# RWKV-7 inverse: the middle products of levels 0 to 3 as sixteen 32x32 blocks in four row sets instead of eight 64x64 blocks in two quarters

## The reference, cut to what matters

```
def step(S, inp):
    r_t, w_t, k_t, v_t, a_t, b_t = inp
    sa = jnp.einsum('bhvk,bhk->bhv', S, a_t)
    S = S * w_t[:, :, None, :] + sa[..., None] * b_t[:, :, None, :] + v_t[..., None] * k_t[:, :, None, :]
    y = jnp.einsum('bhvk,bhk->bhv', S, r_t)
    return S, y
```

## Time and profile before

| | |
|---|---|
| median of three runs | 1392.73 us |
| profiled execution, its time | 1392.75 us |
| its span | 1390.6 us |
| TensorE busy | 1362.9 us, 98% |
| VectorE busy | 855.2 us, 61% |
| ScalarE busy | 696.2 us, 50% |
| line 2782 (the middle products), busy in the core | 25.9 us, 640 records |

### The profile page before, as it was taken

The page is one execution under the profiler, slowest core; times in us unless marked ns, Lnnn a source line. Parts: engine busy times, 40 slices in busy tenths (PEclk is TensorE's granted clock), DMA queues, the critical chain, the costliest instruction groups (busy, mean ns, idle before and its releaser), DMA issues.

```text
span 1390.6 us, 23783 instructions
## 1 busy us (share of the span) xinstructions
PE 1362.9 (98%) x8927; PEld 1118.7 (80%) x8927; DVE 855.2 (61%) x1234; ACT 696.2 (50%) x1110; POOL 38.1 (3%) x42
## 2 busy tenths in 40 slices
PE   9999999999999999999999999899999999999998
PEld 7888877878888878888787688778888887788887
DVE  5455568876755464445784788665555677655554
ACT  5444456675465554444554454235444566644442
POOL 0000000000000000000001000110000010000000
PEclk9999999999999999999999999999999999999999
DMA  8655546555444566555352101315555651266552
GB/s 292 217 181 181 181 145 209 161 191 197 163 158 164 148 203 204 195 183 181 124 187 86 52 4 33 112 46 167 183 192 183 227 174 55 80 214 194 182 184 103
DMA packets 145536, 220.25 MB, mean 158 GB/s; under 512 B 16760, under 2 KB 65294, under 8 KB 145328
## 3 DMA queue, kind: packets, MB, share of 16 engines
q1 hardware_dynamic: 145456, 219.14, 48.4%
HBM read 218.04 MB, written 1.05 MB: 158 GB/s over the span
## 4 chain that ended last, share of the span: by engine, by line
PE 89%; DVE 6%; ACT 3%; issue 1%; POOL 1%; DVEq 0%; POOLq 0%; ACTq 0%
PE acc L291 12%; PE gp L291 12%; PE acc L293 12%; PE acc L292 12%; PE gp L293 12%; PE gp L292 12%; PE tp L952 1%; PE gp L2782 1%; PE acc L2797 1%; DVE sb_w_lo L280 1%; PE acc L1295 1%; PE tp L291 1%; PE tp L293 1%; PE tp L292 1%; PE gp L1884 1%
## 5 line engine op out<-in xcount | busy, mean ns | idle before, releaser
L280 DVE TENSOR_TENSOR sb_w_lo<-sb_raw,sb_w_hi 128x1024 fp32r<-128x1024 f32 (+1 forms) x380 | 451.5, 1214 | 205.2 <-ACT sb_w_hi L264 203.4
L264 ACT ACTIVATE sb_w_hi<-sb_raw 128x1024 fp32r<-128x1024 f32 (+1 forms) x380 | 387.7, 1053 | 207.8 <-PE acc L293 105.9
L291 PE MATMUL gp<-sb_w_hi,sb_xa_hi 128*128 128x512 f32 (+1 forms) x752 | 298.4, 397 | 3.6 <-DVE sb_w_lo L280 2.2
L293 PE MATMUL gp<-sb_w_lo,sb_xa_hi 128*128 128x512 f32 (+1 forms) x752 | 291.7, 388 | 0.0
L292 PE MATMUL gp<-sb_w_hi,sb_xa_lo 128*128 128x512 f32 (+1 forms) x752 | 291.2, 387 | 0.0
L291 PEld LDWEIGHTS gp<-sb_w_hi,sb_xa_hi 128*128 128x128 f32 x752 | 141.3, 188 | 35.7 <-DVE sb_w_lo L280 4.5
L293 PEld LDWEIGHTS gp<-sb_w_lo,sb_xa_hi 128*128 128x128 f32 x752 | 141.2, 188 | 29.6
L292 PEld LDWEIGHTS gp<-sb_w_hi,sb_xa_lo 128*128 128x128 f32 x752 | 141.5, 188 | 27.2 <-issue 0.5
L291 PE MATMUL acc<-sb_w_hi,sb_mid_hi 128*128 128x512 f32 x400 | 156.2, 390 | 0.0
L293 PE MATMUL acc<-sb_w_lo,sb_mid_hi 128*128 128x512 f32 x400 | 155.8, 390 | 0.0
L292 PE MATMUL acc<-sb_w_hi,sb_mid_lo 128*128 128x512 f32 x400 | 155.7, 389 | 0.0
(11 more groups left out here) (417 smaller groups left out, 1758.3 us busy)
## 6 DMA issues: line engine op xcount, KB each, us to landing
sb_raw<-in_ffn_w SPq DMA_DIRECT2D x264, 256.0 KB, 4.4
sb_raw<-in_mlp_w SPq DMA_DIRECT2D x256, 256.0 KB, 2.9
sb_raw<-in_w_in SPq DMA_DIRECT2D x72, 256.0 KB, 3.3
sb_raw<-in_a_w_rkv SPq DMA_DIRECT2D x48, 256.0 KB, 4.1
sb_raw<-in_xattn_w_kv SPq DMA_DIRECT2D x32, 256.0 KB, 3.7
sb_raw<-in_w_out SPq DMA_DIRECT2D x16, 256.0 KB, 3.1
sb_raw<-in_xattn_w_q SPq DMA_DIRECT2D x16, 256.0 KB, 3.0
sb_raw<-in_xattn_w_o SPq DMA_DIRECT2D x16, 256.0 KB, 3.0
```

Of the source, the lines that this page charges most:

```text
L264: A.e.activation(w_hi[:, s, :, 0:n], raw[:, r, :, 0:n], ACT.Copy).then_inc(hi_done, 1)
L280: V.e.tensor_tensor(w_lo[:, s, :, 0:n], raw[:, r, :, 0:n], w_hi[:, s, :, 0:n].bitcast(F32), ALU.subtract).then_inc(lo_done, 1)
L291: e.matmul(dst, xh, wh, start=start, stop=False)
L293: return e.matmul(dst, xh, wl, start=False, stop=stop)
```

## The change: what it does

At level n the mask wants only entries inside diagonal blocks of 2^(n+2), at most 32 for n = 0 to 3. So for these levels only the two 32x32 blocks on the diagonal of each 64x64 product are computed. Each needs only 32 input partitions. `pe_z` then issues sixteen matmuls of 32x32x32 where it issued eight of 64x64x64; in turn they read partitions 0, 64, 32 and 96 onwards and write 64, 0, 96 and 32 onwards. Level 4, whose blocks are 64 wide, is as before. The blocks off the diagonal in `gp` keep what was there; ScalarE still copies all 256 columns, and the masks drop what comes of them. No other instruction is changed.

```diff
+BLOCK = P // 4
...
+            def crossed_blocks(self):
+
+                for col in range(0, HALF, BLOCK):
+                    for at, there in self.crossed():
+                        yield slice(at.start + col, at.start + col + BLOCK), slice(there.start + col, there.start + col + BLOCK), col
...
                 for m in range(4):
-                    for at, there in self.crossed():
-                        mm = T.e.matmul(gp[there, s, m * HALF:(m + 1) * HALF], self.mt[s][at, m, 0, there], self.x_inv[s][at, m, :], start=True, stop=True)
+                    if n < LEVELS - 1:
+                        for at, there, col in self.crossed_blocks():
+                            mm = T.e.matmul(gp[there, s, m * HALF + col:m * HALF + col + BLOCK], self.mt[s][at, m, 0, there],
+                                            self.x_inv[s][at, m, col:col + BLOCK], start=True, stop=True)
+                    else:
+                        for at, there in self.crossed():
+                            mm = T.e.matmul(gp[there, s, m * HALF:(m + 1) * HALF], self.mt[s][at, m, 0, there], self.x_inv[s][at, m, :], start=True, stop=True)
                 mm.then_inc(*T.one(self.z[s]))
```

## The result

The kernel after took 1396.86 us (median of seven runs, 1395.37 to 1398.65), the kernel before 1392.75 (seven runs, 1392.54 to 1395.92). Ratio 1.0024, 95% interval 1.0015 to 1.0033: slower. The forecast was 1389.6 with a range of 1388.4 to 1393.0, and slower had a chance of 0.09. The profiled execution of after took 1395.37, span 1393.2, mean granted clock 0.994.

What follows compares the result with a forecast made beforehand. TensorE was taken as the bound, busy 98% of the span. Savings of 0.44 (unit 0), 2.04 (passes 1 to 4), 0.27 (5 and 6) and 0.43 (7) sum to 3.2 us: 1389.6, range 1388.4 to 1393.0.

Steps and rivals of the forecast that it cites:

- The product: Middle product of levels 0 to 3 on TensorE: 0.46 us instead of 0.68, next shape after 0.39 instead of 0.61.
- the floor: Rival: a short matmul's interval stays that of 64 columns, so nothing is saved; 1392.7 us (to 1393.0), 20%.
- the row sets: Rival: 32x32 tiles in different row sets do not run side by side; +9 us, 1402, 8%.
- The places: Saving at each changed product of a pass, by which wait ends last: 0.54 us a pass, 3.2 us in all.
- Unit 0: First unit, alone with three products: two save in full, the third nothing; 0.44 us saved.
- z(u, 0): Level 0 product in front of level 4's: saves nothing, since xy(3, 0) waits for the second fill-in.
- Levels 2 and 3: Level 2, before the columns, saves 0.22 us a pass; level 3, between pairs and rhs, saves 0.17.
- passes 5 and 6: VectorE's group norm comes between and most of the saving is lost; 0.27 us left for both together.
- pass 7: Last pass: 0.21 us at z(7, 1), nothing at z(7, 2), 0.22 at z(7, 3); 0.43 saved.
- the instruction supply: Rival: 512 more records shift the fetches; a second or doubled stop gives 1390.6 us, none 1388.5; 8% for the first.
- the stop of the earlier trace: TensorE's 0.84 us standstill without a wait in xy(7, 1), DMA engines full; read as a late instruction fetch.
- level 1: Product z(u, 1), followed by u_first and xy(u, 1): saves 0.15 of 0.22 us a pass.

Runs made afterwards that it cites:

- e4: Kernel before with the 32x32 blocks at level 0 only, weight loads not held: 1392.70 us, ratio 1.0001.
- e12: Kernel after with blocks only at levels 2 and 3, and the weight loads held until y of unit 6 is done: 1389.75 us, ratio 0.9976.
- e8: Kernel before, with only the weight loads held until y of unit 6 is done: 1391.92 us, ratio 0.9987.
- e3: Kernel after, all four levels in blocks, with the weight loads held until y of unit 6 is done: 1391.38 us, ratio 0.9982.
- e7: e3 plus 64 small matmuls (256 instructions) in one 32x32 corner at the head of TensorE's program: 1397.85 us, ratio 1.0031.
- e9: e3 plus 32 small matmuls (128 instructions, half a block) in all four row sets at the head of the core: 1392.81 us, ratio 0.9994.
- e10: e8 plus 32 small matmuls (128 instructions, half a block) in all four row sets at the head of the core: 1391.67 us, ratio 0.9989.
- e1: Kernel after plus one unused 128x128x512 matmul in pass 7 between rhs(6) and a_mat(7), filling a TensorE wait: 1397.42 us, ratio 1.0026.
- e2: Kernel after with the 32x32 blocks only in units 0 to 5, units 6 and 7 as before: 1392.62 us, ratio 0.9991.
- e5: e3 with the blocks only at levels 1 to 3, weight loads held: 1391.52 us, ratio 0.9981.
- e11: e6 without the hold, so blocks at level 2 only and weight loads not held: 1394.90 us, ratio 1.0006.
- e6: e3 with the blocks at level 2 only, weight loads held: 1390.88 us, ratio 0.9979.

## Why the prediction was wrong, by its own steps

**The product.** Right in every term: 0.45 us for 0.46, next shape after 0.38 for 0.39, 32 ns between two records of one row set as extrapolated, and the floor and the row sets as rivals both wrong; the matmul records take 191 ns where I had extrapolated 190.

**The places.** Right, a little low. Unit 0: -0.45 for -0.44. z(u, 0): nothing (e4). Levels 2 and 3 have 4 x (0.22 + 0.17 - 0.06) and about 0.2 in passes 5 and 6 and 0.22 in pass 7, 1.7 by the forecast; they measure 2.2 (e12 against e8). Pass 4 without a stop (e3 against e8) is 13.68 for 14.45 us. I held passes 5 and 6 to 0.27 because the group norm would take the rest; after against before it is 0.59 there, with a stop included. The core of e3 less its stops is 3.76 us shorter than e8's, an estimate from above, since a stop can hide a wait. The quickest run of e3, 1388.96, lies 2.96 under the median of e8. So the forecast 3.2 us seem to be there when nothing takes them; the quickest run wasn't profiled, so that it had no stop isn't shown.

**The step that failed: the instruction supply.** I had read the stop of the earlier trace rows as a late fetch, rightly, and priced it at one more stop of about 1 us, 1390.6, with 8% (and with none 1388.5, where 1389.6 less 0.84 is 1388.8). What the runs show is that the 32x32 products at all four levels make stops of about 2 us in the core at both phases that were tried (2.41 and 1.85 in e3 and e7, 2.16 in e9) and 3.17 with the burst, where 64x64 products have none (e8, e10) or, with the burst, 0.84. I had asked how many records are added in all and how they shift the phase of the fetches, and not how fast one stretch uses a block up. xy was already at 32 matmul records in 0.5 us; a new middle product adds 32 records in 0.39 us, where there were 16 in 0.46 to 0.61. At that pace a block would last 2 us or less. It holds only for moments, but the shortest time from edge to edge in the core did fall, from 3.74 us before to 3.04. A fetch takes 0.9 to 1.5 us, and then 1.2 to 1.6 us pass before TensorE goes on, 2.2 to 2.9 together; and the fetches that end a stop start late, 12 to 91 matmul records ahead of it (in e1 even after it has begun). By the edges of the blocks, with DMA full they mostly start 3.4 us or more after TensorE has passed the edge before (3.84 and 3.92 in after; one of e1 at 2.23), without it 1.0 to 2.4 us (once 3.02, in e9). The Trainium skill ("Runtime: NRT & Kernel Launch", Instruction fetch mechanics) says that refills come in blocks of 256 instructions, "mostly hidden", since instructions are issued more slowly than the blocks are filled. The first half agrees with 4 fetches for 1,024 instructions and with the stops at multiples of 256; the second does not hold here, by the 3.17 us. I hadn't weighed it.

**A term that was missing: the clock.** It read 1.00 everywhere before, and I wrote nothing of it. In after it is at half for 13.65 us, of which TensorE stands in stops for 2.0; the other 11.7, at 0.34 to 0.40 us lost for each, are 4.0 to 4.7 us, more than the stops: this is the larger of the two terms. Now the ledger of the core: -3.2 forecast, +2.3 stops (3.17 less 0.84) and +4.0 to +4.7 clock give +3.1 to +3.8, measured +2.62. The places that were sized low are the likely rest: with the -3.76 of above it is +2.6 to +3.3.

**The same stretch, differently.** The earlier trace rows and the stop right behind them named the burst of weights. I took it as scenery. e8 shows that it alone costs before 1.2 us, and holding it gives after 5.5 us. What the burst does is shown in part: in it stops are longer (0.84, 1.44, 1.81 and 3.71 with it, 0.34 or none at the same steps without). A long stop needs no burst, though (1.08 in e3, 1.59 in e9), and neither does a fall (e2, e5, e9).

**Open.** Why a stop falls on some edges and not on others, and why some fetches start late without a burst. And what brings the clock down. Falls come in or behind stops (e1, e2, e5, e7, e9, e11) or behind waits for VectorE (after), but nearly the same waits in e12, and the stop of 1.08 in e3's profiled execution, brought none. The profiled executions of the four kernels without a stop of 0.2 us (e6, e8, e10, e12) have no fall. For their other runs this isn't shown: a mean clock of 0.999, which many of them have, is also that of e5's profiled execution, with a fall of 3.41 us in it, and two runs of e10 lie 2 us above the rest. A rule I can't give.

## What to carry to other kernels

More, smaller instructions can be faster each and still lose: before splitting a matmul, count how many instructions the densest few microseconds will use, and look for idle time ended by "issue" in the middle of a step, which here meant that the stretch was already at the supply's limit. Split only where the wait that ends last is shortened (here levels 2 and 3, and not level 0, which gives nothing, nor level 1, with which the stops came). And before sizing a change by tenths of a microsecond, move away the large transfer that shares its stretch: here one wait on a load queue was worth 5.5 us to the changed kernel and 1.2 to the one before.

## What the runs showed of the hardware

- A 32x32 fp32 product in four row sets: its 32 records start 7 ns apart in fours, a four every 32 ns, and the next shape starts 0.38 us after the first, with 191 ns for one record; a change of shape in front of the next matmul costs no more than between larger tiles. In one 32x32 corner of the array a record follows the other after 31 to 32 ns at full clock and 53 to 55 at half (e7).
- An instruction fetch is 256 instructions, and all 33 stops stand at multiples of 256 records of TensorE, to within one. A fetch takes 0.9 to 1.5 us, and TensorE goes on 1.2 to 1.6 us after it has come in; under full DMA its one packet can start 1.34 us after TensorE has run dry (e1), and the stop is then 3.7 us.
- Half clock lasted 3.41, 6.83 or 13.65 us at a time. On small, latency-bound matmuls a microsecond of it costs 0.34 us (e9 against e3), 0.36 (e11 against e6) or 0.40 (pass 1 of e2 against that of after, stops taken off), not 0.5.
- 64 matmuls of 32x32 in one corner at the head of the program made the start of the core 5.7 us later, 4.78 of it their own time; 32 of them in all four row sets at the head of the core cost nothing that could be measured (1391.67 for 1391.92).
